# MLP output product of a two-layer encoder: seven block products in place of eight, with sums of tokens and weights made on GpSimd

## The chip, the cores and the metric

The kernel runs on one core of a Trainium2 chip. The metric is the device time of one execution in microseconds. A run's time is the span that the profiler sees on the core and some 2 us around it.

## The reference, cut to what matters

Two layers over 256 tokens of 1024 features in float32. Each has attention with gates (not touched here) and then the MLP, which this change is about:

```python
h = rms_norm(x, g_mlp_pre)
h = jnp.square(jax.nn.relu(h @ w_mlp_in)) @ w_mlp_out     # 1024 -> 4096 -> 1024
x = x + rms_norm(h, g_mlp_post)
```

## The kernel before

**Precision.** TensorE works on float32 values cut in two: a high part (a cast to fp32r, which is rounded) and a low part (value less high part). A product of one block is three matmuls: high x high, high x low, low x high. So every weight that arrives is cast by ScalarE (`hi`, into `w_hi`, line 678), has its low part made by VectorE (`lo`, `raw - w_hi`, into `w_lo`, line 1019), and only then goes to TensorE.

**Loads, pieces, rings.** The queue of SyncE brings 64 loads a layer of up to 1 MB into `raw`, four slots in turn. Each load is worked in two pieces, so a layer has 128; `w_hi` and `w_lo` have four slots for pieces of up to 128x1024. ScalarE casts piece p once TensorE has used piece p-4 (`piece_used`); VectorE takes what ScalarE has cast (`hi_ready`); TensorE waits for `lo_ready`; a slot of `raw` is loaded again when the low parts of its last piece are made. Each engine works strictly in the order that its block of the program writes out.

**The MLP.** The hidden width 4096 is cut into eight chunks of 512. For a chunk, the input product makes h transposed (128 hidden features by 256 tokens in each of four PSUM banks, `sc0`, `sc1`, `tp0`, `tp1`; `mlp_in_wide`, lines 1689 to 1703), the two halves of a bank being two partial sums. VectorE adds them out of PSUM (`sum_h`, line 1067), ScalarE takes relu (line 784), GpSimd squares (`square`, line 531), ScalarE and VectorE make high and low parts (`h_hi_of`, line 792; `h_lo_of`, line 1058). The output product (`mlp_out`, through `product`, lines 1380 to 1382) then multiplies h, as the stationary operand, by 512 rows of `w_mlp_out`; it adds up in the banks `acc0` to `acc3` (token tile by column half) over all chunks. Chunks 0 and 1 get h in a way of their own ahead of the loop (`first_product`, `turned_product`). In the loop of five, TensorE takes the input product of chunk j+2 and the output product of chunk j+1 in turn, pieces 76 on; the last pieces follow unrolled. `finish` does the last output product tile by tile, so that the norm after it can begin.

The lines that order one turn of the loop on TensorE:

```python
pe.wait_ge(relu_done, here.count(TT * MJ, 2 * TT, TT))
mlp_in_wide(here, 76)
h_is_split(here, 1)
mlp_out(here, 80)
```

GpSimd does only the squares in this stage, two a chunk. Elsewhere it scales probabilities, applies rotary tables and makes the reciprocal norms.

Of the kernel before, what the change touches and what calls it, by code (L numbers as in the profile page):

```python
# [26 lines left out]
ALU = mybir.AluOpType  # L27
# [38 lines left out]
    + [("out", 4, COL)] * 4 + [("mlp", 4, COL)] * 32)  # L66
NL = len(LOADS)
NP = 2 * NL
# [4 lines left out]
L_LOOP = L_MLP + 6  # L73
LOOP_J = MJ - 3
assert NL == 64 and LOADS[L_MLP][0] == "mlp" and LOADS[L_MLP - 1][0] == "out"

# [7 lines left out]
def piece_rows(p):  # L84

    nk = LOADS[p // 2][1]
    cut = (nk + 1) // 2
    return (0, cut) if p % 2 == 0 else (cut, nk)
# [77 lines left out]
def build(nc, x_d, pos_d, g_mix_pre, g_mix_post, g_mlp_pre, g_mlp_post, w_in, b_gate, sinks_d, q_norm,  # L166
          kv_norm, w_uq, w_ukv, w_oa, w_ob, w_out, w_mlp_in, w_mlp_out, out_d):
    ctx = ExitStack()
    with ctx:
# [3 lines left out]
        def sem(name):  # L173
            return ctx.enter_context(nc.semaphore(name))
# [96 lines left out]
        h_summed = sem("h_summed")  # L271
        h_ready = sem("h_ready")
# [29 lines left out]
        def raw_view(p):  # L302

            n, N = p // 2, LOADS[p // 2][2]
            k0, k1 = piece_rows(p)
            return raw[:, n % RAW, k0 * N:k1 * N]

        def in_order(p, *views):

            if LOADS[p // 2][0] != "ukv":  # L310
                return views
            first, rest = views[0], views[1:]
            return (first.rearrange("p (h c d) -> p c h d", h=4, c=2),
                    *(u.rearrange("p (c h d) -> p c h d", c=2, h=4) for u in rest))

        def split_view(buf, p):
            k0, k1 = piece_rows(p)
            return buf[:, p % RING, 0:(k1 - k0) * LOADS[p // 2][2]]
# [32 lines left out]

        h_banks = sc + tp
# [30 lines left out]
        def _(sp):  # L383
# [8 lines left out]
            def raw_free(pos, n):  # L392

                sp.wait_ge(lo_ready, pos.count(NP, 2 * n + 2, 8))
# [9 lines left out]
            for l in range(DEPTH):  # L404
# [56 lines left out]
                mlp_out(pos, n + 4, 0)  # L461
                with sp.Fori(0, LOOP_J) as j:
                    here = Pos(l, j)
                    mlp_in(here, L_LOOP, j + 2)
                    mlp_out(here, L_LOOP + 2, j + 1)
                n = L_LOOP + 4 * LOOP_J
                mlp_in(pos, n, MJ - 1)
                mlp_out(pos, n + 2, MJ - 2)
                mlp_out(pos, n + 4, MJ - 1)
                assert n + 6 == NL  # L470
# [11 lines left out]
        def _(pool):  # L482
# [41 lines left out]
            def square(pos, j):  # L524

                for t in range(TT):
                    pool.wait_ge(relu_done, pos.count(TT * MJ, TT * j + t + 1, TT))
                    if j > 1:

                        pool.wait_ge(h_split, pos.count(TT * (MJ - 1), TT * (j - 2) + t + 1, TT))  # L530
                    g.tensor_tensor(tok[:, t, 0:COL], relu_h[:, t, :], relu_h[:, t, :], ALU.mult).then_inc(h_ready, 1)  # L531
# [37 lines left out]
            for l in range(DEPTH):  # L569
# [69 lines left out]
                square(pos, 0)  # L639
                square(pos, 1)  # L640
                with pool.Fori(0, LOOP_J) as j:
                    square(Pos(l, j), 2)
                square(pos, MJ - 1)
# [6 lines left out]
        def _(act):  # L650
# [15 lines left out]
            def hi(pos, upto):  # L666

                while state[0] <= upto:
                    p = state[0]
                    n = p // 2  # L670
                    if pos.l == 0 and pos.j is None and p == 0:
                        act.wait_ge(first_loaded, 16)
                    elif p % 2 == 0 or p == 1:
                        loads, in_layer = transfers(n)
                        act.wait_ge(raw_full[n % RAW], pos.count(16 * in_layer, 16 * loads, 16))
                    act.wait_ge(piece_used, pos.count(NP, p + 1, 8))
# [103 lines left out]
            def relu_of_sum(pos, j):  # L780

                for b in range(2):
                    act.wait_ge(h_summed, pos.count(TT * (MJ - 2), TT * (j - 2) + b + 1, TT))
                    s.activation(relu_h[:, b, :], relu_h[:, b, :], ACT.Relu).then_inc(relu_done, 1)  # L784

            def h_hi_of(pos, j, k0, p):

                if p is not None:
                    used(pos, p)
                for b in range(2):  # L790
                    act.wait_ge(h_ready, pos.count(TT * MJ, TT * j + b + 1, TT))
                    s.copy(s2_hi[:, k0 + 2 * b:k0 + 2 * b + 2, :], bank_of_h(tok, b)).then_inc(h_hi, 1)
# [15 lines left out]
            for l in range(DEPTH):  # L808
# [119 lines left out]
                hi(pos, 79)  # L928
                base = 2 * L_LOOP
                assert base == 76  # L930
                with act.Fori(0, LOOP_J) as j:
                    here = Pos(l, j)
                    hi(here, base + 4)

                    h_hi_of(here, 1, 0, base - 1)
                    hi(here, base + 6)
                    relu_of_sum(here, 2)
                    hi(here, base + 11)
                base += 8 * LOOP_J
                state[0] = base + 4  # L940
                hi(pos, base + 4)
                h_hi_of(pos, MJ - 2, 0, base - 1)
                hi(pos, base + 6)
                relu_of_sum(pos, MJ - 1)
                hi(pos, base + 8)
                h_hi_of(pos, MJ - 1, 4, None)
# [19 lines left out]
        def _(dve):  # L966
# [86 lines left out]
            def h_lo_of(pos, j, k0):  # L1053

                for b in range(2):
                    dve.wait_ge(h_hi, pos.count(TT * (MJ - 1), TT * (j - 1) + b + 1, TT))
                    kk = slice(k0 + 2 * b, k0 + 2 * b + 2)
                    v.tensor_tensor(s2_lo[:, kk, :], bank_of_h(tok, b), s2_hi[:, kk, :].bitcast(F32), ALU.subtract)\
                        .then_inc(h_split, 1)

            def sum_h(pos, j, p):
                dve.wait_ge(piece_used, pos.count(NP, RING + p + 1, 8))
                for b in range(2):
                    dve.wait_ge(h_ready, pos.count(TT * MJ, TT * (j - 1) + b + 1, TT))
                    for f in range(2):
                        bank = h_banks[2 * b + f]
                        ins = v.tensor_reduce(relu_h[:, b, f * SEQ:(f + 1) * SEQ],  # L1067
                                              bank[:, :].rearrange("p (a n) -> p n a", a=2), AX, ALU.add)
                    ins.then_inc(h_summed, 1)
# [126 lines left out]
            for l in range(DEPTH):  # L1196
# [133 lines left out]
        def _(pe):  # L1330
# [31 lines left out]
            def product(pos, p, k0, stat, banks, start=False, stop=False, tiles=(0, 1), release=True, mark=None,  # L1362
                        free=None, between=None):
# [3 lines left out]
                N = LOADS[p // 2][2]  # L1367
# [4 lines left out]
                for t in tiles:  # L1372
# [3 lines left out]
                    for k in range(b - a):  # L1376
                        kk = k0 + a + k
                        if k == 0 and between is not None:
                            between()
                        mm(banks[t][:, 0:N], h[:, kk, tk], wh[:, k, :], start=(start and k == 0), stop=False)  # L1380
                        mm(banks[t][:, 0:N], h[:, kk, tk], wl[:, k, :], start=False, stop=False)  # L1381
                        ins = mm(banks[t][:, 0:N], low[:, kk, tk], wh[:, k, :], start=False,  # L1382
                                 stop=(stop and k == b - a - 1))
# [14 lines left out]
            def first_product(pos, p0, kind, turned0=False):  # L1398


                N = LOADS[p0 // 2][2]
# [178 lines left out]
            for l in range(DEPTH):  # L1580
# [95 lines left out]
                def finish(pos, p, k0, stat, before_last=None, within_last=None):  # L1676

                    for t in range(TT):
                        for i in range(4):
                            if t == 1 and i == 3 and before_last is not None:  # L1680
# [3 lines left out]
                                    between=within_last if t == 1 and i == 3 else None)  # L1684
# [4 lines left out]
                def mlp_in_wide(pos, p):  # L1689


                    for i in range(4):
                        pe.wait_ge(lo_ready, pos.count(NP, 2 * RAW + p + i + 1, 8))
                        wh, wl = (split_view(w, p + i).rearrange("p (k n) -> p k n", k=2) for w in (w_hi, w_lo))
                        for f in range(4):
                            bank, cols = h_banks[f], slice(f * P, (f + 1) * P)
                            for k in range(2):
                                mm(bank[:, :].rearrange("p (a n) -> p a n", a=2), wh[:, k, cols], s1_both[:, :, 2 * i + k, :],  # L1698
                                   start=(i == 0 and k == 0), stop=False)
                            for k in range(2):  # L1700
                                ins = mm(bank[:, SEQ:2 * SEQ], wl[:, k, cols], s1_hi[:, 2 * i + k, :], start=False,  # L1701
                                         stop=(i == 3 and k == 1))
                        ins.then_inc(piece_used, 1)
# [52 lines left out]
```

## Time and profile before

| | |
|---|---|
| median of 3 runs | 753.39 us (753.14 to 753.55) |
| profiled execution | 753.48 us, span 751.5 us |
| mean granted TensorE clock | 0.998 of 2.4 GHz |
| TensorE busy | 740.3 us, 99% |
| VectorE busy | 505.8 us, 67% |
| ScalarE busy | 414.4 us, 55% |
| GpSimd busy | 158.6 us, 21% |
| read from HBM | 130.59 MB |

Busy time of an engine is time in which at least one of its instructions runs. Matmuls overlap in the record, so a matmul's duration is longer than its pace; the pace is read from starts. An instruction that waits for a port after it was issued counts as busy.

### The profile page before, as it was taken

What the parts mean: (1) busy time and instruction counts of PE and PEld (TensorE: products, weight loads), DVE (VectorE), ACT (ScalarE), POOL (GpSimd) and SP (SyncE); (2) the same over time, 40 slices, a digit from 0 to 9 for tenths busy, and PEclk for the clock granted to TensorE, in tenths of its full rate; (3) what the DMA queues carried; (4) which work ended last, traced back from release to release, by engine and by line L of the source; (5) the groups of instructions that cost most, each with busy time, mean ns of one, the idle gap of its engine ahead of it and who ended that gap; (6) DMA issues with size and microseconds to landing.
All of it is one profiled execution on the core that took longest, in us unless ns stands there. A gap on an engine that the chain in (4) does not pass through costs nothing.

```text
span 751.5 us, 11313 instructions
## 1 busy us (share of the span) xinstructions
PE 740.3 (99%) x4194; PEld 640.3 (85%) x4194; DVE 505.8 (67%) x678; ACT 414.4 (55%) x779; POOL 158.6 (21%) x262
## 2 busy tenths in 40 slices
PE   8999999999999999999999999999999999999996
PEld 7999887888798888888889997888888988888885
DVE  5878777567765656656686887766668566565674
ACT  6867665434664544444576866644447444554452
POOL 1990433000130111110128414220003210011110
PEclk9999999999999999999999999999999999999999
DMA  7866633565465545466338584335473656555511
GB/s 260 208 205 218 220 113 115 167 215 168 129 215 178 213 170 193 156 207 211 105 114 242 182 281 144 113 117 194 139 223 121 220 164 223 189 202 176 202 71 56
DMA packets 79501, 132.19 MB, mean 176 GB/s; under 512 B 15290, under 2 KB 21476, under 8 KB 79204
## 3 DMA queue, kind: packets, MB, share of 16 engines
q1 hardware_dynamic: 79188, 131.64, 53.7%
q8 instruction: 26, 0.43, 0.2%
q14 instruction: 15, 0.12, 0.0%
q10 hardware_dynamic: 272, 0.00, 0.0%
HBM read 130.59 MB, written 1.05 MB: 175 GB/s over the span
## 4 chain that ended last, share of the span: by engine, by line
PE 91%; DVE 3%; ACT 2%; POOL 1%; DMA 1%; issue 1%; SPq 0%; POOLq 0%; ACTq 0%; DVEq 0%
PE acc L1380 15%; PE acc L1382 15%; PE acc L1381 15%; PE tp L1698 6%; PE sc L1698 6%; PE acc L1414 4%; PE tp L1355 3%; PE tp L1701 3%; PE sc L1701 3%; PE sc L1516 2%; PE sc L1457 2%; PE sc L1455 2%; PE sc L1456 2%; PE sc L1380 2%; PE sc L1381 1%; PE sc L1382 1%
## 5 line engine op out<-in xcount | busy, mean ns | idle before, releaser
L1019 DVE TENSOR_TENSOR w_lo<-raw,w_hi 128x1024 fp32r<-128x1024 f32 (+4 forms) x256 | 306.0, 1216 | 162.5 <-ACT w_hi L678 161.0
L678 ACT CAST w_hi<-raw 128x1024 fp32r<-128x1024 f32 (+4 forms) x256 | 251.5, 997 | 177.7 <-PE acc L1382 94.3
L1380 PE MATMUL acc<-w_hi,s_hi 128*128 128x512 f32 x288 | 112.2, 390 | 0.0
L1381 PE MATMUL acc<-w_lo,s_hi 128*128 128x512 f32 x288 | 112.1, 389 | 0.0
L1382 PE MATMUL acc<-w_hi,s_lo 128*128 128x512 f32 x288 | 112.0, 389 | 0.0
L1380 PE MATMUL acc<-w_hi,s_both 128*128 128x512 f32 (+2 forms) x256 | 95.5, 373 | 0.0
L1382 PE MATMUL acc<-w_hi,s_both 128*128 128x512 f32 (+2 forms) x256 | 93.4, 365 | 0.0
L1381 PE MATMUL acc<-w_lo,s_both 128*128 128x512 f32 (+2 forms) x256 | 93.3, 364 | 0.0
L531 POOL TENSOR_TENSOR tok<-relu_h 128x512 f32<-128x512 f32 x32 | 37.0, 1161 | 263.6 <-ACT relu_h L784 241.6
L1382 PEld LDWEIGHTS acc<-w_hi,s_lo 128*128 128x128 f32 x288 | 54.1, 188 | 11.3
L1380 PEld LDWEIGHTS acc<-w_hi,s_hi 128*128 128x128 f32 x288 | 54.1, 188 | 10.8
L1381 PEld LDWEIGHTS acc<-w_lo,s_hi 128*128 128x128 f32 x288 | 54.1, 188 | 10.6
L1698 PE MATMUL tp<-s_both,w_hi 128*128 128x512 f32 x192 | 60.3, 395 | 0.0
L1698 PE MATMUL sc<-s_both,w_hi 128*128 128x512 f32 x192 | 60.2, 395 | 0.0
L802 ACT ACTIVATE probs<-sc,neg_m 128x128 f32<-128x128 f32 (+2 forms) x96 | 35.2, 390 | 40.0 <-DVE neg_m L1137 22.0
L1382 PEld LDWEIGHTS acc<-w_hi,s_both 128*128 128x128 f32 x256 | 48.2, 188 | 7.8
L1380 PEld LDWEIGHTS acc<-w_hi,s_both 128*128 128x128 f32 x256 | 48.2, 188 | 7.4 <-DVE w_lo L1019 0.4
L1381 PEld LDWEIGHTS acc<-w_lo,s_both 128*128 128x128 f32 x256 | 48.3, 189 | 6.9
L514 POOL TENSOR_TENSOR var<-sums,norm_k 128x1 f32<-128x1 f32 x24 | 8.5, 354 | 186.9 <-ACT squares L740 186.7
L1701 PEld LDWEIGHTS tp<-s_both,w_lo 128*128 128x128 f32 x192 | 36.1, 188 | 8.5
L1701 PEld LDWEIGHTS sc<-s_both,w_lo 128*128 128x128 f32 x192 | 36.1, 188 | 8.4
L784 ACT ACTIVATE relu_h<-relu_h 128x512 f32<-128x512 f32 x24 | 15.2, 632 | 44.0 <-DVE relu_h L1067 44.0
(212 smaller groups left out, 1337.6 us busy)
## 6 DMA issues: line engine op xcount, KB each, us to landing
raw<-in_w_mlp_in SPq DMA_DIRECT2D x32, 1024.0 KB, 5.3
raw<-in_w_mlp_out SPq DMA_DIRECT2D x32, 1024.0 KB, 5.0
raw<-in_w_in SPq DMA_DIRECT2D x24, 1024.0 KB, 5.3
raw<-in_w_oa SPq DMA_DIRECT2D x8, 1024.0 KB, 5.0
raw<-in_w_out SPq DMA_DIRECT2D x8, 1024.0 KB, 5.0
raw<-in_w_ob SPq DMA_DIRECT2D x4, 1024.0 KB, 4.9
raw<-in_w_in SPq DMA_DIRECT2D x3, 768.0 KB, 4.9
raw<-in_w_in SPq DMA_DIRECT2D x4, 576.0 KB, 6.5
```

The source lines that it names most:

```text
L531: g.tensor_tensor(tok[:, t, 0:COL], relu_h[:, t, :], relu_h[:, t, :], ALU.mult).then_inc(h_ready, 1)
L678: s.copy(high, src).then_inc(hi_ready, 1)
L784: s.activation(relu_h[:, b, :], relu_h[:, b, :], ACT.Relu).then_inc(relu_done, 1)
L802: ins = s.activation(probs[:, i % 2, a * w:(a + 1) * w], sc[i % 2][:, a * w:(a + 1) * w], ACT.Exp, bias=neg_m[:, c + a:c + a + 1], scale=S ...
L1019: v.tensor_tensor(low, src, high, ALU.subtract).then_inc(lo_ready, 1)
L1355: ins = nc.tensor.transpose(b[0:rows, i * P:(i + 1) * P], src, ident[:, :])
L1380: mm(banks[t][:, 0:N], h[:, kk, tk], wh[:, k, :], start=(start and k == 0), stop=False)
L1381: mm(banks[t][:, 0:N], h[:, kk, tk], wl[:, k, :], start=False, stop=False)
L1382: ins = mm(banks[t][:, 0:N], low[:, kk, tk], wh[:, k, :], start=False, stop=(stop and k == b - a - 1))
L1414: ins = mm(acc[t][:, 0:N], xs[:, 2 * i + k, t * P:(t + 1) * P], w[:, k, :], start=(first and i == 0 and k == 0), stop=(last and i == 3 and ...
L1698: mm(bank[:, :].rearrange("p (a n) -> p a n", a=2), wh[:, k, cols], s1_both[:, :, 2 * i + k, :], start=(i == 0 and k == 0), stop=False)
L1701: ins = mm(bank[:, SEQ:2 * SEQ], wl[:, k, cols], s1_hi[:, 2 * i + k, :], start=False, stop=(i == 3 and k == 1))
```

## The change

For chunks 1 to 6 the output product is done in blocks of two by two. A half chunk (256 hidden features) of squared h is a matrix of 2 x 2 blocks (hidden features by token tiles, a12 and so on), and the 256 rows of `w_mlp_out` a matrix of 2 x 2 blocks of 128 x 512. In place of eight block products there are seven, between sums of blocks of h and sums of blocks of weights, which add up over twelve halves in seven banks (`acc0` to `acc3`, `sc0`, `sc1`, `tp0`); at the end the four results are combined out of them.

- The weight sums, four blocks of 128x512 a half, are made by GpSimd from `raw` into `gate_a` and `gate_b` (`weight_sums`, three instructions). The token sums are made by GpSimd with the squares (`square_and_sum`, six instructions in place of one, into seven blocks of 128x128). All of them are cut into high and low parts by ScalarE and VectorE as the rest is.
- A load of a half is one of 256 columns of `w_mlp_in` (1 KB rows, all eight row blocks) and one of 256 rows of `w_mlp_out`. A half has six pieces: `in0`, `low`, `first`, `in1`, `t13`, `t24`; `first` has 512 elements a partition, the others 1024.
- The input product is done a block of 128 hidden features at a time, in the one bank `tp1` (the first half has `tp0` too), which VectorE empties block by block (`sum_h`) before the next can begin.
- The output products of chunk 0 and chunk 7 stay as they were, and are both done last, on top of the combined banks. The combination is a copy by ScalarE and seven additions by VectorE.
- The loops of the MLP are written out; nothing loops.

The core of the diff:

```diff
-    + [("out", 4, COL)] * 4 + [("mlp", 4, COL)] * 32)
+    + [("out", 4, COL)] * 4 + [("mlp", 4, COL)] * 4 + [("in", KD, SEQ), ("pair", 2, D)] * 12 + [("mlp", 4, COL)] * 4)
...
+NHALF = 2 * (MJ - 2)
+P_PAIR = 2 * L_PAIR
+P_LAST = P_PAIR + 6 * NHALF
...
+def half_order(s):
+    if s == 0:
+        return ("in0", "in1", "low", "first", "t13", "t24")
+    if s == NHALF - 1:
+        return ("in0", "low", "first", "t13", "t24", "in1")
+    return ("in0", "low", "first", "in1", "t13", "t24")
...
+SUM_A = {"a11": 0, "a12": 1, "a22": 2, "s4": 3, "s1": 4, "s2": 5, "s3": 6}
...
+            def square_and_sum(pos, j, b):
+                relu_ready(pos, j, b)
+                tile = tok[:, b, :].rearrange("p (s n) -> p s n", n=P)
+                ka = relu_h[:, b, 0:SEQ].rearrange("p (t n) -> p t n", t=TT)[:, ::-1, :]
+                kb = relu_h[:, b, SEQ:2 * SEQ].rearrange("p (t n) -> p t n", t=TT)
+                g.tensor_tensor(tile[:, 0:2, :], ka, ka, ALU.mult)
+                sums_a.link(g.tensor_tensor(tile[:, 2:4, :], kb, kb, ALU.mult))
+                g.tensor_tensor(tile[:, 7, :], tile[:, 1, :], tile[:, 0, :], ALU.subtract)
+                sums_a.link(g.tensor_tensor(tile[:, 5, :], tile[:, 0, :], tile[:, 3, :], ALU.add))
+                sums_a.link(g.tensor_tensor(tile[:, 6, :], tile[:, 5, :], tile[:, 1, :], ALU.subtract))
+                g.tensor_tensor(tile[:, 4, :], tile[:, 2, :], tile[:, 6, :], ALU.subtract).then_inc(h_ready, 1)
+            def weight_sums(pos, s):
...
+                pool.wait_ge(raw_full[n % RAW], pos.count(16 * in_layer, 16 * loads))
+                if s >= 2:
+                    pool.wait_ge(lo_ready, pos.count(NP, 2 * RAW + half_piece(s - 2, "t24") + 1))
...
+                g.tensor_tensor(made[:, 0:2, :], block[:, 1::2, :], block[:, 0:2, :], ALU.subtract).then_inc(t_made, 1)
+                pool.wait_ge(t_made, at(1))
+                g.tensor_tensor(made[:, 2, :], block[:, 3, :], made[:, 0, :], ALU.subtract).then_inc(t_made, 1)
+                pool.wait_ge(t_made, at(2))
+                g.tensor_tensor(made[:, 3, :], block[:, 2, :], made[:, 2, :], ALU.subtract).then_inc(t_made, 1)
...
+                weight_sums(pos, 0)
+                for b in range(2):
+                    square_and_sum(pos, 1, b)
+                weight_sums(pos, 1)
+                for s in range(NHALF):
...
+                        square_and_sum(pos, j, b)
...
+                    if s + 2 < NHALF:
+                        weight_sums(pos, s + 2)
```

ScalarE's, VectorE's and TensorE's order for one half in the middle (`half`, with p its first piece):

```diff
+                    hi(pos, p + 4)
+                    pair_high(pos, *half_of(half - 1))
+                    hi(pos, p + 7)
+                    relu_of_sum(pos, half)
+                    hi(pos, p + 9)
...
+                    sum_h(pos, half, 0)
+                    lo(pos, p + 4)
+                    pair_low(pos, *half_of(half - 1))
+                    lo(pos, p + 6)
+                    sum_h(pos, half, 1)
+                    lo(pos, p + 9)
...
+                    in_piece(pos, half, 0)
+                    pair_low(pos, half)
+                    pair_first(pos, half)
+                    in_piece(pos, half, 1)
+                    pair_t13(pos, half)
+                    pair_t24(pos, half)
```

TensorE's pieces: `pair_low` has two block products (a12 into `acc0`, s4 into `acc2`), `pair_first` one (a11 into `sc0`), `pair_t13` two (s1 into `acc3`, s3 into `tp0`), `pair_t24` two (s2 into `sc1`, a22 into `acc1`), each of three matmuls of 512 columns:

```diff
+                pe.wait_ge(lo_ready, pos.count(NP, 2 * RAW + p + 1))
+                    if s > 0:
+                        pe.wait_ge(h_summed, pos.count(2 * NHALF, 2 * s + f))
...
+                        mm(bank[:, :], pair_hi[b][:, tk], wh[:, i, :], start=first, stop=False)
+                        mm(bank[:, :], pair_hi[b][:, tk], wl[:, i, :], start=False, stop=False)
+                        ins = mm(bank[:, :], pair_lo[b][:, tk], wh[:, i, :], start=False, stop=last)
```

## Rows read from the trace of the kernel before

**Rows 1.** The page: span, busy time of each engine, the chain that ended last.
```profile
span 751.5 us, 11313 instructions
PE 740.3 (99%) x4194; PEld 640.3 (85%) x4194; DVE 505.8 (67%) x678; ACT 414.4 (55%) x779; POOL 158.6 (21%) x262
...
PE 91%; DVE 3%; ACT 2%; POOL 1%; DMA 1%; issue 1%; SPq 0%; POOLq 0%; ACTq 0%; DVEq 0%
```

**Rows 2.** Windows: start:end, length, busy (instructions) by engine, clock, DMA share, GB/s.
```profile
core 0: us, PE busy (x) PEld busy (x) DVE busy (x) ACT busy (x) POOL busy (x), PEclk, DMA share, GB/s
0.00:4.00 4.00, 1.39 (x6) 1.36 (x7) 0.97 (x6) 1.49 (x2) 1.83 (x41) 1.00 0.38 94
...
234.10:256.13 22.03, 22.03 (x114) 18.74 (x113) 13.39 (x14) 10.52 (x13) 2.08 (x2) 1.00 0.54 189
```

**Rows 3.** Timeline, TensorE in the loop: start, length, engine, line, operation, count.
```profile
263.48 0.63 PE L1698 MATMUL tp<-s_both,w_hi 128*128 128x512 f32 x2
...
264.18 0.63 PE L1698 MATMUL sc<-s_both,w_hi 128*128 128x512 f32 x2
...
266.96 0.40 PE L1380 MATMUL acc<-w_hi,s_hi 128*128 128x512 f32 x1
...
277.62 0.39 PE L1382 MATMUL acc<-w_hi,s_lo 128*128 128x512 f32 x1
```

**Rows 4.** Groups by line and shape, one period: count, busy us, mean ns, idle before.
```profile
L1019 DVE TENSOR_TENSOR w_lo<-raw,w_hi 128x1024 fp32r<-128x1024 f32 x8 | 9.7, 1232 | 8.0 <-ACT w_hi L678 8.0
L678 ACT CAST w_hi<-raw 128x1024 fp32r<-128x1024 f32 x9 | 9.4, 1050 | 9.4 <-PE acc L1382 5.3 <-PE tp L1701 4.2
...
L531 POOL TENSOR_TENSOR tok<-relu_h 128x512 f32<-128x512 f32 x2 | 2.1, 1042 | 21.7 <-ACT relu_h L784 21.5
L1067 DVE TENSOR_REDUCE relu_h<-sc 128x256 f32<-128x512 f32 x2 | 1.3, 686 | 0.6 <-PE tp L1701 0.6
L1058 DVE TENSOR_TENSOR s_lo<-tok,s_hi 128x512 fp32r<-128x512 f32 x2 | 1.3, 684 | 0.0
...
L784 ACT ACTIVATE relu_h<-relu_h 128x512 f32<-128x512 f32 x2 | 1.3, 632 | 3.7 <-DVE relu_h L1067 3.7
L792 ACT CAST s_hi<-tok 128x512 fp32r<-128x512 f32 x2 | 1.1, 616 | 0.0
```

**Rows 5.** Two GpSimd lines: duration in ns, minimum/median/maximum.
```profile
L590 POOL TENSOR_TENSOR latent<-latent,rstd x8: 616/1070/1591, 29.4 to 401.3; 128x384 f32<-128x384 f32 x4, 128x256 f32<-128x256 f32 x4
...
L600 POOL TENSOR_TENSOR gate_a<-cost,rstd x4: 395/402/1386, 37.8 to 403.5; 128x128 f32<-128x128 f32 x4
```

**Rows 6.** Timeline of VectorE and of GpSimd, 208 to 217 us.
```profile
209.13 3.50 DVE L1019 TENSOR_TENSOR w_lo<-raw,w_hi 128x1024 fp32r<-128x1024 f32 x3 [1.95 <-ACT w_hi L678]
212.95 3.64 DVE L1019 TENSOR_TENSOR w_lo<-raw,w_hi 128x1024 fp32r<-128x1024 f32 x2 [0.32 <-ACT w_hi L678]
...
211.56 3.94 POOL L531 TENSOR_TENSOR tok<-relu_h 128x512 f32<-128x512 f32 x2 [2.31 <-ACT relu_h L778]
```

**Rows 7.** Timeline of VectorE and of GpSimd, 49 to 56 us.
```profile
49.69 2.79 DVE L1090 TENSOR_TENSOR qT_a<-acc,tok 64x512 f32<-64x512 f32 x4
52.51 3.11 DVE L1019 TENSOR_TENSOR w_lo<-raw,w_hi 128x1024 fp32r<-128x1024 f32 x2
...
51.28 0.74 POOL L377 TENSOR_TENSOR gate_b<-gate_b,gate_a 128x256 f32<-128x256 f32 x1
...
52.92 1.61 POOL L376 TENSOR_TENSOR gate_b<-gate_b,cost 128x256 f32<-128x256 f32 x1
```

**Rows 8.** Timeline at the end of piece 71, start of the stage changed.
```profile
222.77 0.28 PE L1457 MATMUL sc<-s_both,w_lo 128*128 128x256 f32 x1
...
223.09 1.09 ACT L778 ACTIVATE relu_h<-sc 128x512 f32<-128x512 f32 x2 [1.78 <-PE sc L1457]
...
223.77 2.04 POOL L531 TENSOR_TENSOR tok<-relu_h 128x512 f32<-128x512 f32 x2 [8.27 <-ACT relu_h L778]
...
225.15 3.06 DVE L1019 TENSOR_TENSOR w_lo<-raw,w_hi 128x1024 fp32r<-128x1024 f32 x2 [2.58 <-ACT w_hi L678]
```

**Rows 9.** DMA issues: count, KB each, median us to landing.
```profile
raw<-in_w_mlp_out SPq DMA_DIRECT2D x32, 1024.0 KB, 5.0
...
raw<-in_w_in SPq DMA_DIRECT2D x4, 512.0 KB, 4.2
```

More of the change, by code:

```diff
@@ L302, in raw_view @@
         def raw_view(p):
-            n, N = p // 2, LOADS[p // 2][2]
+            n, part = PIECES[p]
+            kind, nk, N = LOADS[n]
+            if kind == "in":
+                cols = slice(0, P) if part == "in0" else slice(P, 2 * P)
+                return raw[:, n % RAW, :].rearrange("p (k n) -> p k n", k=KD)[:, :, cols]
+            if kind == "pair":
+                s = (n - L_PAIR) // 2
+                return {"low": raw[:, n % RAW, D:2 * D], "first": raw[:, n % RAW, 0:COL],
+                        "t13": t_buf[s % 2][:, 0:D], "t24": t_buf[s % 2][:, D:2 * D]}[part]
             k0, k1 = piece_rows(p)
@@ L522, in pool_rope, with relu_ready @@
                 return rope(g, steps, gate_a[:, 1, 0:COL], q, heads, half, t, stride)
[L524 to L531, printed above, removed]
+            def relu_ready(pos, j, b):
+                pool.wait_ge(relu_done, pos.count(TT * MJ, TT * j + b + 1))
+                if j > 1:
+                    pool.wait_ge(h_split, pos.count(TT * (MJ - 1), TT * (j - 2) + b + 1))
@@ L778, in relu, with relu_of_sum, pair_high, last_high @@
                     s.activation(relu_h[:, t, :], banks[t][:, :], ACT.Relu).then_inc(relu_done, 1)
[L780 to L792, printed above, removed]
+            def relu_of_sum(pos, s):
+                b = half_of(s)[1]
+                act.wait_ge(h_summed, pos.count(2 * NHALF, 2 * s + 2))
+                nc.scalar.activation(relu_h[:, b, :], relu_h[:, b, :], ACT.Relu).then_inc(relu_done, 1)
+            def pair_high(pos, j, b):
+                act.wait_ge(h_ready, pos.count(TT * MJ, TT * j + b + 1))
+                if j > 1:
+                    used(pos, half_piece(2 * (j - 2) + b, "t24"))
+                s.copy(pair_hi[b], tok[:, b, P:D]).then_inc(h_hi, 1)
+            def last_high(pos, b):
+                act.wait_ge(h_ready, pos.count(TT * MJ, TT * (MJ - 1) + b + 1))
+                used(pos, half_piece(NHALF - 2, "t24"))
+                s.copy(yb_hi[:, 2 * b:2 * b + 2, :], bank_of_h(tok, b)).then_inc(h_hi, 1)
+            def copy_p1(pos):
+                used(pos, half_piece(NHALF - 1, "first"))
+                s.copy(probsT[:, 0, :], sc[0][:, :]).then_inc(p1_copied, 1)
             def exps(pos, i):
@@ L927, in _ @@
                 relu(pos, 1, 71, sc)
[L928 to L946, printed above, removed]
+                hi(pos, P_PAIR + 3)
+                pair_high(pos, 1, 0)
+                hi(pos, P_PAIR + 5)
+                pair_high(pos, 1, 1)
+                relu_of_sum(pos, 0)
+                hi(pos, P_PAIR + 9)
+                for half in range(1, NHALF - 1):
+                    p = P_PAIR + 6 * half
+                    hi(pos, p + 4)
[3 more added lines that the diff above has]
+                    hi(pos, p + 9)
+                hi(pos, P_LAST - 2)
+                last_high(pos, 0)
+                hi(pos, P_LAST)
+                copy_p1(pos)
+                hi(pos, P_LAST + 3)
+                relu_of_sum(pos, NHALF - 1)
+                hi(pos, P_LAST + 4)
+                last_high(pos, 1)
                 hi(pos, NP - 1)
@@ L1683, in finish @@
                                     mark=tile0_done if i % 2 == 1 else None,
-                                    between=within_last if t == 1 and i == 3 else None)
+                                    between=within_last if t == 1 and i == 3 else None, seeded=seeded)
                 finish(pos, 60, 4, s1, lambda: turn_x(pos, "xm", 0))
[L1689 to L1703, printed above, removed]
@@ new lines, in pair_low, with pair_first, pair_t13, pair_t24 @@
+                def pair_low(pos, s):
+                    pe.wait_ge(h_split, pos.count(TT * (MJ - 1), s + 1))
+                    pair_piece(pos, s, "low", (("a12", acc[0]), ("s4", acc[2])))
+                def pair_first(pos, s):
+                    pair_piece(pos, s, "first", (("a11", sc[0]),))
+                def pair_t13(pos, s):
+                    pair_piece(pos, s, "t13", (("s1", acc[3]), ("s3", tp[0])))
+                def pair_t24(pos, s):
+                    pair_piece(pos, s, "t24", (("s2", sc[1]), ("a22", acc[1])))
@@ L1727, in _ @@
-                h_is_split(pos, MJ - 2)
+                in_piece(pos, 0, 0)
+                in_piece(pos, 0, 1)
+                pair_low(pos, 0)
+                pe.wait_ge(relu_done, pos.count(TT * MJ, 2 * TT))
+                pair_first(pos, 0)
+                pe.wait_ge(h_summed, pos.count(2 * NHALF, 2))
+                pair_t13(pos, 0)
+                pair_t24(pos, 0)
+                for half in range(1, NHALF - 1):
+                    in_piece(pos, half, 0)
[4 more added lines that the diff above has]
+                    pair_t24(pos, half)
@@ L1728, in _, with whole @@
+                half = NHALF - 1
+                in_piece(pos, half, 0)
+                pair_low(pos, half)
+                pair_first(pos, half)
+                pair_t13(pos, half)
+                pair_t24(pos, half)
+                in_piece(pos, half, 1)
+                def whole(c):
+                    return lambda t: pe.wait_ge(combined, pos.count(7, (1, 4, 6, 7)[2 * c + t]))
                 for i in range(4):
-                    product(pos, base + 4 + i, 0, s2, pair[i // 2])
-                h_is_split(pos, MJ - 1)
+                    product(pos, P_LAST + i, 0, s2, pair[i // 2], free=whole(i // 2) if i % 2 == 0 else None, seeded=True)
```

234 lines of the change are left out of this document (148 added, 86 removed).

## The prediction

> **What bounds the kernel now.** I read the page first: TensorE is busy for 740.3 of 751.5 us and stands for 91% of the chain that ended last [rows 1]. Then the loop of the MLP stage, cut at its period: 22.03 us a chunk, TensorE busy in all of it at a granted clock of 1.00, which is 2.4 GHz, while VectorE is busy 13.39 us, ScalarE 10.52 and GpSimd 2.08 [rows 2]. So before the change every product taken away is worth its own pace. That pace is read from starts, since durations overlap: 48 output products from 266.96 to the start of the last at 277.62, 10.66 us over 47 steps, 0.2268 us each; four input products (two of 512 columns, two of 256) every 0.70 us, 2.79 us for a piece of sixteen [rows 3]. 48 x 0.2268 + 4 x 2.79 = 22.03, the period.
>
> **TensorE's side.** A half of a chunk costs 24 output products now and 7 x 3 = 21 after, and the same input work. Half: 2 x 2.79 + 21 x 0.2268 = 10.33 us against 11.01. Over twelve halves and two layers: 72 x 0.2268 = 16.3 us off. Chunk 0's output product (48 x 0.2268 = 10.88 us) is only moved to the end of the stage.
>
> **What is added elsewhere, a half.** Durations of the loop [rows 4].
> - ScalarE: casts of in0, in1, low, t13, t24 (5 x 1.05), of first (0.62), of the seven block sums (896 elements, between 0.62 and 1.05: 0.95), a relu of 0.63: 7.5 us. Not the bound, but in the chain below.
> - VectorE: five lows of 1.23, one of 512 (0.68), low of the block sums (896: 1.09), two reductions of 0.68: 9.3 us, against 6.7 before.
> - GpSimd: one tensor_tensor of 1024 elements and two of 512 for the weight sums, two of 256 and four of 128 for the token sums. Rows: 128 elements 0.40, 256 0.62 (the minimum of each line), 512 1.04, so 1.67 ns an element, and 1024 is put at 1.90 [rows 4, 5]. Sum 1.90 + 2 x 1.04 + 2 x 0.62 + 4 x 0.40 = 6.8 us, against 1.04 before.
>
> Taken singly, 7.5, 9.3 and 6.8 all lie beneath 10.33, and the change would look hidden. It isn't, because VectorE and GpSimd do not run at the same time here.
>
> **The step that decides.** At 209.13 three lows take 3.50 us, 1.17 each. From 212.95 two take 3.64, and the two squares of GpSimd at 211.56 take 3.94 in place of 2.08 [rows 6]. The times fit only turns: low ends 212.63, square 1 ends about 213.5, low about 214.7, square 2 at 215.50, low at 216.59. From 212.63 to 216.59 is two squares and two lows, 1.98 us a pair: a square adds 0.79 us to VectorE's stream. The same with other shapes: a GpSimd operation of 256 elements takes 0.74 beside a VectorE operation that reads PSUM (49.69) and 1.61 beside lows from SBUF (52.51) [rows 7]. So a VectorE operation with both inputs in SBUF and a GpSimd one exclude each other for their whole length; reductions out of PSUM do not take part.
>
> The Trainium skill (SBUF — State Buffer, SBUF: two separate sides) says so: the pair of ports that the two share is an exclusive lock, a VectorE operation with two SBUF inputs takes it against a GpSimd one that reads SBUF, and the loser waits for the whole instruction. By this rule, the trace agrees, 1.61 against 0.74.
>
> Per half the shared part is: lows and block sums 5 x 1.19 + 0.65 + 1.05 = 7.6 us (in series), GpSimd 3072 elements at 0.79 us for 512 = 4.7 us. Together 12.3 us, over TensorE's 10.33 and over the 11.01 of before. That is the lower bound if everything fits; with hand-over counted at nothing it would be 11.9 (3072 x 1.67 ns = 5.1, and VectorE's elements 6528 in 6.8 us at 1024 in 1.07, the last low of rows 6 after its wait). Upper side: VectorE's 9.0 in series plus all 4.7 is 13.7 if nothing of GpSimd falls under the two reductions.
>
> Order makes it tend to the upper side. A ring of dependence runs from one relu_of_sum to the next: square_and_sum on GpSimd, pair_high on ScalarE, and then on VectorE, in its fixed order, pair_low, lo of t24, lo of the next in0, sum_h, and the relu again. With turns: 0.16 to start; six GpSimd operations (3.1 us with three waits on themselves) between which the lows of low, first and in1 get in, about 5.5; pair_high 1.05 with its wait; then weight_sums of the next half holds the port, started at once: 0.6 left of its 1.6, pair_low 1.0, 0.8, lo 1.1, 0.8, lo 1.1; sum_h 0.7; relu 0.75. Sum 13.6 us. Without turns the same ring is 0.16 + 3.1 + 1.05 + 1.1 + 1.2 + 1.2 + 0.7 + 0.75 = 9.3 us, under 10.33. I take 13.3 us a half, between 12.3 and 13.6 and nearer the ring, since it holds in-order waits that the mere sum leaves out.
>
> Weight sums are wanted by ScalarE two halves later and are not late; TensorE waits 3 us a half, in two places: ahead of t24 and ahead of in0 (its lo, and the single bank tp[1] that sum_h has to empty).
>
> The Trainium skill (GPSIMD Engine Reference, 3.1 Elementwise — side-by-side cycle accounting) puts the floor of a two-input operation at about 2.5 cycles an element, some 2.1 ns; an estimate from the page is 6.4 us of GpSimd for 3072 elements and some 1.5 us more a half, 840 us in all. The row has 2.0 cycles (1.04 us for 512), and the row is used.
>
> **Start and end of the stage.** Layer 0: TensorE is through with piece 71 at 223.0 [rows 8] and now has only in0(0) and in1(0) to cover the way of chunk 1's h, where before it had mlp_out(0). Relu's first tile 223.8, six sums with a low of rows 8 between 228.0, pair_high 229.1, pair_low 230.6: TensorE, done at 228.6, waits 2.0. low, first, t13, t24 end at 235.4; the second tile's sums end at 233.0, pair_high 234.1, relu 234.7, cast 235.8, lo behind pair_low and a weight sum 237.9: 2.5 more. Without these waits in0(1) would start at 233.35; I have 237.9. GpSimd's work ends two halves early, so the ring holds for ten steps; then a half at TensorE's pace, 10.33, and chunks 0 and 7, 96 x 0.2268 = 21.8. There seven adds of 0.68 and a copy on VectorE and ScalarE (5.4 us) lie beneath in1 and the first products and cost nothing; without that cover they would be 5 us a layer.
>
> Sum: 237.9 + 10 x 13.3 + 10.33 + 21.8 = 403.0, against 223.0 + 10.88 + 132.2 + 10.88 = 377.0. 26.0 later, 52 in two layers. 751.5 + 52 = 803.5 span; the profiled execution was 753.48 and the median is 753.39, so **805 us**. The stage breaks even at 10.7 us a half.
>
> **Edits at nothing.** Loads: the input block has 1 KB rows. The 512 KB loads with such rows land in 4.2 us, 1024 KB with longer rows in 5.0 [rows 9]; doubled at most 8.4 for the one, with 5.0 for the other, inside the 13 us, and each is issued a half or more ahead. Were they in series against 10.33 they would give 13.4 too, so this bound changes nothing. Unrolled loops, a view with another order, two new banks (sc) as sums: no row has a price; at nothing, since TensorE now has 3 us a half to spare.
>
> **Rivals.**
> - TensorE stays the bound (faster). For it: every engine alone is below 10.33, and the ring without turns is 9.3. Then in0(1) at 234.2, and 234.2 + 10 x 10.33 + 32.1 = 369.6: 7.4 earlier a layer, 739 us (745 with the start's waits). Against it: 11.9 us of work that rows 6 and 7 show taking turns. Chance 0.08.
> - Turns, but all fits (slower): 12.3 a half or a little below, the ring loosened since GpSimd's sums fall beneath reductions: 237.9 + 123 + 32.1 = 393.0, 785 us. In the range; 0.25 with its neighbourhood down to 776.
> - The forecast, 12.6 to 14.2 a half, 790 to 824: 0.55.
> - Clock: TensorE idles 3 of 13 us a half and could be granted 1.2 GHz; its half would be near 20 us and the time 753 + 20 x 9, over 900 if throughout, 830 to 850 if now and then. Against it: in the first 4 us TensorE is busy 1.39 at a granted clock of 1.00 [rows 2]. With longer turns than I count, 0.10 above 830.
> - The remainder, 0.02, is between 745 and 776.
>
> So faster 0.08, same 0.01, slower 0.91 (0.2% is about what a measurement here tells from no change), and the range 776 to 830 leaves 0.2 out.
>
> **What would show it.** Right: in the stage GpSimd's 128x1024 operations of 1.9 us and its small ones take a low's length more, lows stretch to 1.8 to 2.8, VectorE is busy over 90% of a half; TensorE has gaps before t24 and in0 ended by w_lo; a half is 13 us; the last half and chunks 0 and 7 run gapless. Wrong: a half at 10.3 with TensorE gapless, or the gaps ended by raw, or a clock under 1.00. What would make me wrong: a shorter hold of the port by small GpSimd operations, or turns given in another order than strictly one by one.

## The result, and the profile after

The changed kernel takes 841.81 us (median of 4 runs, 841.34 to 843.53) against 753.47 before: ratio 1.1177, 95% interval [1.1158, 1.1197]. I had forecast 805, with a range of 776 to 830: the direction was right, the size was not, and the time lies outside the range.

The page of the changed kernel: span and busy time, the granted clock in 40 slices, the chain by engine, and one group of lows.

```profile
span 841.8 us, 11101 instructions
PE 757.3 (90%) x4122; PEld 637.9 (76%) x4122; DVE 659.7 (78%) x740; ACT 455.3 (54%) x829; POOL 416.7 (49%) x454
...
PEclk9999999999998989899999999999999799999989
...
PE 54%; DVE 21%; POOL 15%; ACT 6%; issue 3%; POOLq 0%; ACTq 0%; DVEq 0%
...
L1141 DVE TENSOR_TENSOR w_lo<-gate_a,w_hi 128x1024 fp32r<-128x1024 f32 x24 | 44.4, 1852 | 2.1 <-ACT w_hi L788 1.8
```

TensorE's share of the chain fell from 91% [rows 1] to 54%, and VectorE with GpSimd has 36%. A low of 1.23 us [rows 4] takes 1.85 on average where its source is a weight sum in `gate_a` (1.72 where it is one in `gate_b`). Now one half of the new loop, from relu to relu, in the changed kernel's timeline of VectorE, ScalarE, GpSimd and the first matmul after the gap.

```profile
283.95 3.79 DVE L1141 TENSOR_TENSOR w_lo<-raw,w_hi 128x1024 fp32r<-128x1024 f32 x3
284.07 0.63 ACT L894 ACTIVATE relu_h<-relu_h 128x512 f32<-128x512 f32 x1 [4.58 <-DVE relu_h L1192]
...
284.78 0.86 POOL L606 TENSOR_TENSOR tok<-relu_h 128x256 f32<-128x256 f32 x1 [2.43 <-ACT relu_h L894]
285.60 1.06 POOL L607 TENSOR_TENSOR tok<-relu_h 128x256 f32<-128x256 f32 x1
286.74 1.32 POOL L608 TENSOR_TENSOR tok<-tok 128x128 f32<-128x128 f32 x1
...
290.01 0.46 POOL L611 TENSOR_TENSOR tok<-tok 128x128 f32<-128x128 f32 x1
290.43 2.40 POOL L624 TENSOR_TENSOR gate_b<-raw 128x1024 f32<-128x1024 f32 x1
290.50 0.95 ACT L901 CAST s_hi<-tok 128x896 fp32r<-128x896 f32 x1 [2.15 <-POOL tok L611]
...
291.48 2.29 DVE L1178 TENSOR_TENSOR s_lo<-tok,s_hi 128x896 fp32r<-128x896 f32 x1 [1.87 <-ACT s_hi L901]
...
292.91 1.99 POOL L626 TENSOR_TENSOR gate_b<-raw,gate_b 128x512 f32<-128x512 f32 x1
293.70 2.28 DVE L1141 TENSOR_TENSOR w_lo<-gate_a,w_hi 128x1024 fp32r<-128x1024 f32 x1
294.98 2.15 POOL L628 TENSOR_TENSOR gate_b<-raw,gate_b 128x512 f32<-128x512 f32 x1
295.90 2.30 DVE L1141 TENSOR_TENSOR w_lo<-raw,w_hi 128x1024 fp32r<-128x1024 f32 x1
...
296.04 0.50 PE L1865 MATMUL sc<-w_hi,yb_hi 128*128 128x512 f32 x1 [2.62 <-DVE w_lo L1141]
298.13 0.68 DVE L1192 TENSOR_REDUCE relu_h<-tp 128x256 f32<-128x512 f32 x1
...
298.84 0.63 ACT L894 ACTIVATE relu_h<-relu_h 128x512 f32<-128x512 f32 x1 [4.56 <-DVE relu_h L1192]
```

Read it as a relay. The token sums run 284.78 to 290.47 (5.7 us; their own durations and gaps would be 3.3); the first weight sum holds the port until 292.8, so the low of the block sums, issued at 291.48, lasts 2.29; then weight sum, low, weight sum, low in strict turns, each low 2.3; sum_h; relu. The chain of this stretch names the same steps in this order, with no other between them. TensorE waits 2.62 us for the low of t24 and then for sum_h to empty the bank. VectorE is busy for 12.76 of the 14.77 us, 86%, where I had expected over 90%.

### The profile page after: what moved, and what is told of

Same layout as the page of the kernel before. It is cut to its first block, busy times and chain, and to the rows that moved or that the text cites. A ratio compares the mean times of both kernels' runs of the same rounds, so it can differ in the third digit from the quotient of the medians.

```text
span 841.8 us, 11101 instructions
## 1 busy us (share of the span) xinstructions
PE 757.3 (90%) x4122; PEld 637.9 (76%) x4122; DVE 659.7 (78%) x740; ACT 455.3 (54%) x829; POOL 416.7 (49%) x454
## 4 chain that ended last, share of the span: by engine, by line
PE 54%; DVE 21%; POOL 15%; ACT 6%; issue 3%; POOLq 0%; ACTq 0%; DVEq 0%
DVE w_lo L1141 14%; PE acc L1530 8%; PE acc L1533 8%; PE acc L1532 8%; PE acc L1565 3%; POOL tok L608 3%; PE tp L1505 3%; PE tp L1850 2%; POOL tok L610 2%; POOL tok L607 2%; DVE yb_lo L1178 2%; POOL tok L606 2%; PE sc L1667 2%; PE sc L1608 2%; PE sc L1606 2%
## 5 line engine op out<-in xcount | busy, mean ns | idle before, releaser
L1141 DVE TENSOR_TENSOR w_lo<-raw,w_hi 128x1024 fp32r<-128x1024 f32 (+4 forms) x256 | 333.5, 1321 | 57.5 <-ACT w_hi L788 54.3
L1850 PE MATMUL tp<-s_both,w_hi 128*128 128x512 f32 x384 | 134.2, 434 | 24.0 <-DVE relu_h L1192 15.8
L1850 PEld LDWEIGHTS tp<-s_both,w_hi 128*128 128x128 f32 x384 | 66.5, 209 | 36.9 <-DVE w_lo L1141 32.9
L1853 PEld LDWEIGHTS tp<-s_both,w_lo 128*128 128x128 f32 x384 | 79.3, 207 | 19.6
L1853 PE MATMUL tp<-s_both,w_lo 128*128 128x256 f32 x384 | 80.8, 294 | 0.0
L662 POOL TENSOR_TENSOR probs<-probs,denom 128x512 f32<-128x512 f32 x26 | 28.9, 1114 | 41.8 <-DVE denom L1235 41.8
L1141 DVE TENSOR_TENSOR w_lo<-gate_a,w_hi 128x1024 fp32r<-128x1024 f32 x24 | 44.4, 1852 | 2.1 <-ACT w_hi L788 1.8
L1141 DVE TENSOR_TENSOR w_lo<-gate_b,w_hi 128x1024 fp32r<-128x1024 f32 x24 | 41.3, 1720 | 3.0 <-ACT w_hi L788 2.7
L1192 DVE TENSOR_REDUCE relu_h<-tp 128x256 f32<-128x512 f32 x48 | 32.7, 682 | 12.4 <-PE tp L1853 6.6
L1178 DVE TENSOR_TENSOR s_lo<-tok,s_hi 128x896 fp32r<-128x896 f32 x12 | 27.2, 2269 | 15.2 <-ACT s_hi L901 15.2
```

What stands on the lines that cost most here:

```text
L662: g.tensor_tensor(view, view, denom[:, c:c + n].unsqueeze(2).to_broadcast([P, n, w]), ALU.mult).then_inc(probs_scaled, 1)
L1141: v.tensor_tensor(low, src, high, ALU.subtract).then_inc(lo_ready, 1)
L1178: v.tensor_tensor(pair_lo[b], tok[:, b, P:D], pair_hi[b].bitcast(F32), ALU.subtract).then_inc(h_split, 1)
L1192: v.tensor_reduce(relu_h[:, b, f * SEQ:(f + 1) * SEQ], in_bank(s, f)[:, :].rearrange("p (a n) -> p n a", a=2), AX, ALU.add).then_inc(h_sum ...
L1850: mm(bank[:, :].rearrange("p (a n) -> p a n", a=2), wh[:, kk, :], s1_both[:, :, kk, :], start=(kk == 0), stop=False)
L1853: ins = mm(bank[:, SEQ:2 * SEQ], wl[:, kk, :], s1_hi[:, kk, :], start=False, stop=(kk == KD - 1))
```

## The experiments

Times are medians of 4 runs (e7: 10); each ratio is against the kernel before on the same chip. "Half" is the mean distance of relu_of_sum from the second to the eleventh in layer 0 of the profiled run (nine steps).

| kernel | time, us | ratio, 95% interval | half, us |
|---|---|---|---|
| the change | 841.81 | 1.1177 [1.1158, 1.1197] | 14.86 |
| e1 no GpSimd sums | 738.69 | 0.9805 [0.9788, 0.9821] | 10.33 |
| e2 no weight sums | 762.42 | 1.0121 [1.0105, 1.0138] | 11.22 |
| e3 no token sums | 801.95 | 1.0637 [1.0620, 1.0655] | 13.12 |
| e4 one operand twice | 819.85 | 1.0886 [1.0867, 1.0904] | 13.85 |
| e5 low of block sums later | 825.01 | 1.0952 [1.0934, 1.0971] | 13.93 |
| e6 before, with reads | 803.79 | 1.0672 [1.0654, 1.0689] | |
| e7 before, with memsets | 753.21 | 0.9999 [0.9990, 1.0009] | |
| e8 weight sums on VectorE | 801.27 | 1.0638 [1.0620, 1.0656] | 12.79 |
| e9 and squares on ScalarE | 801.39 | 1.0630 [1.0613, 1.0648] | 12.89 |
| e10 and the order of e5 | 782.25 | 1.0382 [1.0365, 1.0399] | 11.89 |

**e1: everything of the change but GpSimd's sums.** It drops the calls of `weight_sums` and four lines of `square_and_sum`:

```diff
-                  "t13": t_buf[s % 2][:, 0:D], "t24": t_buf[s % 2][:, D:2 * D]
+                  "t13": raw[:, n % RAW, 0:D], "t24": raw[:, n % RAW, D:2 * D]
...
-                g.tensor_tensor(tile[:, 7, :], tile[:, 1, :], tile[:, 0, :], ALU.subtract)
...
-                    if s + 2 < NHALF:
-                        weight_sums(pos, s + 2)
```

> The changed kernel without GpSimd's sums: no weight sums (t13 and t24 are cast straight from raw) and no token sums (squares only, two operations of 256 elements); seven products, the single bank tp1, the 1 KB rows, all casts and lows stay. The output products are then of other blocks. If turns at the port are the whole loss, a half is TensorE's 10.33 us and the time 739 to 745. If the single bank, the loads, the longer list of VectorE or a lower clock have a part of their own, it stays above 760.

738.69 us, and two halves in its windows:

```profile
core 0: us, PE busy (x) PEld busy (x) DVE busy (x) ACT busy (x) POOL busy (x), PEclk, DMA share, GB/s
294.54:304.87 10.33, 10.33 (x54) 8.80 (x53) 9.12 (x10) 7.04 (x8) 1.89 (x2) 1.00 0.65 203
304.87:315.20 10.33, 10.33 (x54) 8.81 (x53) 9.11 (x10) 7.05 (x8) 1.89 (x2) 1.00 0.65 203
```

TensorE has no gap, and 10.33 us is the half of the prediction to the last digit. So the single bank, the loads with short rows, the written-out loops, ScalarE's and VectorE's added casts and lows and the combination at the end cost nothing that lasts; the saving on TensorE is real (14.7 us, of 16.3 counted), and the loss is all in what GpSimd was given. e1 takes away the waits for the sums together with the work, so it doesn't tell the port from the waits; e6 and e7 do.

**e2: the weight sums alone taken away** (the first and last part of the diff above).

> The changed kernel without the weight sums alone (t13 and t24 cast from raw); token sums stay. Turns at the port: the ring loses what weight sums hold, 3 to 3.5 of its 14.8 us, so a half is 11.3 to 12.0 us and the time 770 to 785. If GpSimd's weight sums are not what delays the lows (a bank, a load), above 830.

762.42, 8 us under the expected range, with a mean half of 11.22, just under its lower end (the first ones are shorter, the later ones 11.37). The token sums alone cost 24 us over e1. Their way through the ring, in the timeline:

```profile
302.53 0.63 ACT L887 ACTIVATE relu_h<-relu_h 128x512 f32<-128x512 f32 x1 [1.18 <-DVE relu_h L1185]
...
308.43 0.46 POOL L611 TENSOR_TENSOR tok<-tok 128x128 f32<-128x128 f32 x1
...
309.90 1.09 DVE L1171 TENSOR_TENSOR yb_lo<-tok,yb_hi 128x896 fp32r<-128x896 f32 x1 [1.87 <-ACT yb_hi L894]
310.91 2.36 DVE L1134 TENSOR_TENSOR w_lo<-raw,w_hi 128x1024 fp32r<-128x1024 f32 x2
...
313.90 0.63 ACT L887 ACTIVATE relu_h<-relu_h 128x512 f32<-128x512 f32 x1 [1.19 <-DVE relu_h L1185]
```

The lows are back at 1.09 and 1.18, since no weight sum stands between them, yet this half is 11.37: VectorE idles 1.87 us inside the ring. Here it is the ring, not the sum of the work, that binds.

**e3: token sums taken away, weight sums kept.**

> The changed kernel without the token sums (GpSimd squares only, two operations in place of six; the block sums are stale); weight sums stay. Two readings of the turns: if the sum of what is held at the port sets the half (7.6 of VectorE, 4.7 to 5 of weight sums, 1 of squares), 13.3 to 13.5 us and 808 to 814; if only the ring from relu to relu does, 10.8 and 760 to 765. No turns: no change from 842.

801.95, a half of 13.12: neither reading alone, and the nearness to the sum is no evidence for it. In this run the weight sum waits for its own load, 0.46 to 0.82 us in every half of the steady stretch, and a third ring, through the load, has this length:

```profile
300.24 0.37 SPq L464 DMA_DIRECT2D raw<-in_w_mlp_out  x1
...
305.39 2.52 POOL L620 TENSOR_TENSOR gate_b<-raw 128x1024 f32<-128x1024 f32 x1 [0.82 <-DMA raw<-in_w_mlp_out]
...
306.29 2.71 DVE L1137 TENSOR_TENSOR w_lo<-gate_a,w_hi 128x1024 fp32r<-128x1024 f32 x1
...
308.93 2.17 DVE L1174 TENSOR_TENSOR s_lo<-tok,s_hi 128x896 fp32r<-128x896 f32 x1
...
311.02 2.28 DVE L1137 TENSOR_TENSOR w_lo<-gate_a,w_hi 128x1024 fp32r<-128x1024 f32 x1
...
313.33 0.37 SPq L464 DMA_DIRECT2D raw<-in_w_mlp_out  x1
```

The low of t24 frees the slot of `raw`; the next load is issued at 300.24; the weight sum begins at 305.39 and ends at 307.91; three lows follow, each held by a weight sum, and the last of them, that of t24, ends at 313.30; the next load is issued at 313.33, 13.09 us after the first. In the changed kernel the same load is issued at 281.23 and its weight sum starts only at 290.43, so there the load is not last. e3 thus shows that the weight sums hold the lows, but it can't decide between the two readings.

**e4: the price of a GpSimd operation.** Weight sums that read one block as both inputs:

```diff
-  g.tensor_tensor(made[:, 0:2, :], block[:, 1::2, :], block[:, 0:2, :], ALU.subtract)
+  g.tensor_tensor(made[:, 0:2, :], block[:, 1::2, :], block[:, 1::2, :], ALU.add)
```

and so the other two.

> The changed kernel with weight sums that read the same elements as both inputs (twice a block of raw in place of a difference; the values are other ones), same number and size of operations. If my term was off since two different inputs cost GpSimd 2.17 ns an element (2.40 us for 1024 alone) and one input read twice 1.67, these operations fall to 1.90 and 1.04, the port is held 1.4 us less a half, 13.4 us a half and 808 to 816. If the extra 1.6 us a half over my 13.3 come from elsewhere (clock, casts, bank), the time stays within 5 us of 842.

819.85: 22.0 us off, or 1.10 a half, where 26 to 34 were expected. Durations by line (minimum/median/maximum in ns), first the change, then e4:

```profile
L624 POOL TENSOR_TENSOR gate_a<-raw x12: 2401/2407/3380, 215.3 to 777.7; 128x1024 f32<-128x1024 f32 x12
L626 POOL TENSOR_TENSOR gate_a<-raw,gate_a x12: 1286/1996/2162, 218.7 to 780.1; 128x512 f32<-128x512 f32 x12
```

```profile
L624 POOL TENSOR_TENSOR gate_a<-raw x12: 1891/1894/2872, 215.1 to 756.9; 128x1024 f32<-128x1024 f32 x12
L626 POOL TENSOR_TENSOR gate_a<-raw x12: 1040/1767/1769, 218.1 to 758.9; 128x512 f32<-128x512 f32 x12
```

Same sizes, same number, only the second input differs: 2.40 against 1.89, and 1.29 (the minimum, without a wait for the port) against 1.04. Line 624 of the change reads two blocks of the one tensor `raw`, so it isn't a matter of two tensors. (add in place of subtract is a second difference; the squares are a multiply and have 1.04 too.)

**e5: ring or sum.** The complete kernel with one line moved:

```diff
                     sum_h(pos, half, 0)
                     lo(pos, p + 4)
-                    pair_low(pos, *half_of(half - 1))
                     lo(pos, p + 6)
                     sum_h(pos, half, 1)
+                    pair_low(pos, *half_of(half - 1))
```

> The changed kernel, complete, with one line moved in VectorE's order: the low of the block sums comes after sum_h(half, 1) in place of ahead of the lows of t24 and in0, so that it is no longer in the ring from relu to relu. If the sum of what is held at the port sets the half (7.6 of VectorE, 4.6 of weight sums, 2.2 of token sums: 14.4 us), the time stays near, 834 to 842. If the ring does, it is 1.2 us or more shorter and the time 800 to 818.

825.01, between the two ranges: the order is worth 16.8 us (0.93 a half), so the sum of the holds was not the bound, and my 14.4 for it was too high. The ring is shorter but not gone. ScalarE, in its fixed order, still casts t24 only after pair_high, and VectorE waits for that cast:

```profile
302.69 0.94 ACT L901 CAST yb_hi<-tok 128x896 fp32r<-128x896 f32 x1 [3.42 <-POOL tok L611]
303.54 1.04 ACT L788 CAST w_hi<-gate_b 128x1024 fp32r<-128x1024 f32 x1
...
304.61 1.49 DVE L1141 TENSOR_TENSOR w_lo<-gate_b,w_hi 128x1024 fp32r<-128x1024 f32 x1 [2.28 <-ACT w_hi L788]
```

**e6 and e7: the port without any of the change's waits.** The kernel before, with work on GpSimd that nobody waits for, in each turn of the loop; e7 has `g.memset` of 1024 elements sixteen times in the same place.

```diff
+                    for _ in range(3):
+                        extra.link(g.tensor_tensor(gate_b[:, 0, :], gate_a[:, 0, :], gate_a[:, 1, :], ALU.subtract))
+                        extra.link(g.tensor_tensor(gate_b[:, 1, 0:COL], gate_a[:, 0, 0:COL], gate_a[:, 1, 0:COL], ALU.subtract))
+                        extra.link(g.tensor_tensor(gate_b[:, 1, COL:D], gate_a[:, 0, COL:D], gate_a[:, 1, COL:D], ALU.subtract))
```

> The kernel before, complete, with work for GpSimd that nobody waits for: in each of the five turns of the loop three times a subtraction of 1024 elements and two of 512, from gate_a into gate_b (both idle in this stage). GpSimd then runs about 17 of 22.03 us. Turns at the port: 10.8 of VectorE, 1.6 of squares and 3 x 4.6 are 26.2 us a turn of the loop, so 795 us or more. If the change loses by its waits and order and not by the port, nothing here waits for the added work: within 2 us of before.

> As the run before, with sixteen memsets of 1024 elements into gate_b in place of the subtractions: GpSimd is as busy but reads nothing from SBUF. If only operations of GpSimd that read SBUF take turns with VectorE's two-input ones, no change from before, within 2 us. If any GpSimd work does, over 780.

Windows of e6 and then of e7, the second one period of before:

```profile
262.00:287.00 25.00, 22.04 (x109) 17.87 (x108) 23.36 (x14) 9.61 (x12) 21.27 (x11) 1.00 0.47 149
```

```profile
256.13:278.16 22.03, 22.03 (x114) 18.74 (x113) 13.37 (x14) 10.52 (x13) 17.32 (x19) 1.00 0.57 191
```

e6 costs 50.5 us (795 us or more was expected, and it took 803.79) though no instruction of the MLP waits for what was added. The squares stand behind it in GpSimd's order, but they weren't late by it: GpSimd was idle for 3.08 us ahead of the squares at 274.64. e7 has GpSimd busy for 17.32 us a period in place of 2.08 [rows 2] and changes neither the period nor VectorE's 13.4 us. So it is not enough that GpSimd works. What the subtractions do and the memsets don't is to read SBUF and to calculate; no run has one without the other. A low beside a memset, in e7's timeline, takes 1.23:

```profile
276.25 1.22 DVE L1025 TENSOR_TENSOR w_lo<-raw,w_hi 128x1024 fp32r<-128x1024 f32 x1 [1.49 <-ACT w_hi L684]
276.36 0.95 POOL L648 MEMSET gate_b<- 128x1024 f32 x1
```

**e8, e9, e10: can it be repaired?** Complete kernels. e8 makes the weight sums on VectorE, between the lows of `first` and `in1` of the next half; e9 also makes the squares on ScalarE; e10 also has e5's order.

```diff
+                    lo(pos, p + 8)
+                    weight_sums(pos, half + 1)
                     lo(pos, p + 9)
```

> The changed kernel, complete, with the weight sums made by VectorE (1.2 + 2 x 0.65 = 2.5 us a half) in place of GpSimd (5.1 us alone, 4.6 held); the token sums stay on GpSimd. Turns at the port: a half 12.0 to 13.0 us, 775 to 795: better than the change, still over before, since VectorE with 11.5 us in series is now itself over 10.33. If the port were not the cause, more work for VectorE gives more than 842.

> Complete kernel: weight sums on VectorE as in the run before, and the squares of the token sums made by ScalarE (two Square activations into the blocks, some 0.4 us each), so that GpSimd keeps four operations of 128 elements a half, 1.9 us. Turns at the port: GpSimd holds 1 us less and the ring is 1 to 1.5 us shorter; a half 11.8 to 12.5 us, 775 to 795. If the GpSimd operations that are left are not what costs, within 3 us of 801.

> Complete kernel: as the run before, and the low of the block sums after sum_h(half, 1) as in the earlier run of that order. VectorE then has 11.6 us of work in series a half, and that is the bound if the turns are nearly gone: 11.7 to 12.3 us a half, 772 to 786. It should not beat 753: break-even is 10.7.

e8 gains 40.5 us over the change, though VectorE is given 3.3 us more a half (1.63 + 2 x 0.84; I had expected 2.5); it missed its range by 6 us. From 276.15 to 288.61, one half, VectorE is busy for 12.31 of 12.46 us. e9 missed its range too: 801.39 is no gain over e8, which is the other branch of what I expected. In its timeline pair_high comes right behind the cast of t13, at 307.38, and that cast waited 1.48 us for VectorE's weight sum; the token sums were done at 306.7, so taking squares off GpSimd shortened nothing that was last. That is read from one half; I did not test it alone. e10 has a half of 11.89, inside its range, with VectorE busy for 11.81 of it. It is the best complete version of the change, and 3.8% slower than before.

## Why the prediction was wrong, point by point

**The mechanism held.** TensorE's half of 10.33 us (e1, exact), turns at the port for operations that read SBUF on both sides (e6, e7), the ring from relu to relu (the chain of the stretch, e5), TensorE's two gaps ahead of t24 and in0, and the start of the stage: in0(1) began at 238.45, forecast 237.9. Rival "TensorE stays the bound" with its 739 us is what e1 measures once the sums are gone.

**The step that failed** is the price of GpSimd's operations, as I put it: "Rows: 128 elements 0.40, 256 0.62 (the minimum of each line), 512 1.04, so 1.67 ns an element, and 1024 is put at 1.90." These rows are squares and scalings by a broadcast value. A weight sum reads two different blocks and takes 2.40 for 1024 and 1.29 for 512, 2.2 ns an element. The 0.79 us that I let each 512 elements hold the port comes from squares as well. In my ring the three lows behind weight sums are 0.6 + 1.0 + 0.8 + 1.1 + 0.8 + 1.1 = 5.4 us; in the half shown they run from 291.48 to 298.20, 6.7 us, and in e4 the same three take 5.8 (287.32 to 293.08). A row of the right kind stood in my own list: 0.74 for 256 elements with two tensors [rows 7] against 0.62 [rows 5], and I used it only as a proof of turns. e4 prices the error at 22.0 us of the 36.8 by which I was off. It leaves the four block sums of 128 elements as they are; they read two different blocks too and take 0.46 where I had 0.40, some 0.2 us a half (an estimate, 4 x 0.06).

The Trainium skill (GPSIMD Engine Reference, 3.1 Elementwise — side-by-side cycle accounting) has about 2.6 cycles an element for tensor_tensor, as the floor for two inputs; I weighed such a price, at 2.5, gave 840 us as its result, and set it aside for the 2.0 cycles of the square. By this rule, the traces agree for two different inputs, (2.40 - 1.29) us over 512 elements is 2.2 ns, an estimate of 2.6 cycles at the page's 1.2 GHz; with one input read twice the run shows 1.7 ns. That the 840 came so near is in part luck: it charged the squares with the price of two inputs, which they don't have, and my "some 1.5 us more a half" over twenty steps is 835, not 840.

**The rest**, in layer 0: ten steps from in0(1) at 238.45 to in0(11) at 388.09 are 14.96 us each, 1.66 over my 13.3. A half at full clock is 14.77, and 13.80 in e4: 0.97 is the price of the weight sums. 13.80 is 0.20 over the 13.6 that I had worked out for the ring. I took 13.3 as a compromise with the sum: 0.3 more; with this order of work the ring was the longer of the two, so the compromise had no ground. The last 0.19 is a first step of 15.9 us and three halves of 15.0 in which the clock was low. The end of the stage took 34.1 us after in0(11), forecast 32.1. 0.7 of that stands in the kernel before as well, whose stage ended at 377.73 for my 377.0, and e1 takes 33.4 for the same stretch. The 0.7 left over e1 was not taken apart.

**The clock**, which I gave a rival of its own, came in small. Windows of the changed kernel around the gap at 293.4 to 296.0:

```profile
293.00:296.00 3.00, 0.42 (x2) 0.00 (x0) 3.00 (x3) 1.29 (x2) 2.92 (x2) 1.00 0.00 0
296.00:298.90 2.90, 2.15 (x6) 1.20 (x6) 2.90 (x3) 0.06 (x1) 1.12 (x1) 0.67 0.65 162
298.90:301.00 2.10, 2.04 (x6) 1.78 (x7) 2.02 (x3) 2.03 (x3) 1.45 (x2) 0.50 0.67 275
301.00:304.30 3.30, 3.30 (x14) 2.77 (x13) 1.57 (x2) 0.00 (x0) 3.06 (x6) 0.57 0.18 33
```

After 2.6 us of idling the granted clock falls to the lower level, 1.2 GHz, for most of the 8 us from 296.0, and in0, 2.79 us at the full clock, lasts until 304.25. That half is 15.02 us, the one before it 14.77, so most of it lay beneath the ring. Not every such gap is followed by this: of the six gaps of 2.6 us in layer 0, three were, and after the one that ended at 281.25 the clock stayed at 1.00. The rival's 830 to 850 us hold the measured time, and a clock under 1.00 was one of my signs of being wrong; both by luck, since three halves of 0.25 us a layer are under 2 us. What put the time above 830 is what I had added to that rival, "longer turns than I count". The row that I held against this rival, a full clock in the first 4 us with little work, was the wrong kind of row: it says nothing of what follows a gap in a busy stretch.

## What to carry to other kernels

Add up what shares a port before what shares an engine: 9.3, 7.5 and 6.8 us beneath a bound of 10.33 looked free, and the two that take turns were not. Price an operation by a row with the same number of different inputs, and when a row of the wrong kind and a stated rule disagree, look for the row of the right kind first. When work is handed round several in-order engines, write down the ring from a step to its next self: it bounds the period even where every engine and the port have time left (e2). When a part is taken away to see what it costs, look for the ring that is longest then: in e3 it was one that the full kernel doesn't wait for.

## What the runs showed of the hardware that I had not expected

- GpSimd's tensor_tensor in float32 costs more when its two inputs are different: 1024 elements in 2.40 us from two blocks, 1.89 from one block read twice (e4). A broadcast column as the second input costs no more than one block read twice: 256 elements in 0.62 [rows 5].
- A GpSimd memset of 1024 elements, 0.96 us, does not hold up VectorE's two-input operations at all (sixteen a period, time ratio 0.9999).
- Moving 5 us of GpSimd work onto the busier VectorE, where it takes 3.3, made the kernel 40 us faster (e8).
